# Loading expert weights in runs of 32 KB and 16 KB, with every fourth column on the other side of the product

## The reference, cut to what matters

```python
def expert_block(args):
    tok, e = args
    xb = x_pad[tok]
    gu = xb @ w_gu[e] + b_gu[e]            # w_gu[e]: 1024 x 2048 float32, 8 MB
    gate, up = gu[:, :D_FF], gu[:, D_FF:]
    gate = jnp.minimum(gate, SWIGLU_LIMIT)
    up = jnp.clip(up, -SWIGLU_LIMIT, SWIGLU_LIMIT)
    h = (up + 1.0) * gate * jax.nn.sigmoid(SWIGLU_ALPHA * gate)
    return h @ w_down[e] + b_down[e]       # w_down[e]: 1024 x 1024 float32, 4 MB
```

## Time and profile before

| | us |
|---|---|
| median of 3 runs (1173.86 to 1175.33) | 1174.92 |
| the profiled execution, its own time | 1173.83 |
| its span in the trace | 1171.8 |
| PE busy | 1109.4 |
| DVE busy | 298.5 |
| ACT busy | 151.8 |
| POOL busy | 96.4 |

### The profile page before, as it was taken

How to read it: one execution, slowest core, us unless ns; L and a number is a source line. 1 busy time by engine, 2 the same in 40 slices (tenths; PEclk the granted TensorE clock), 3 DMA queues, 4 the chain that set the end, 5 groups by cost and what they waited for, 6 DMA issues and landing times.

```text
span 1171.8 us, 13786 instructions
## 1 busy us (share of the span) xinstructions
PE 1109.4 (95%) x5376; PEld 521.9 (45%) x5376; DVE 298.5 (25%) x529; ACT 151.8 (13%) x245; POOL 96.4 (8%) x53
## 2 busy tenths in 40 slices
PE   8989999899999999999999898989899999999996
PEld 5879955535343434343434242424242424243432
DVE  3771664421212121121202020211112121212113
ACT  3242101011101011111010111111101010110101
POOL 3684420000000000000000000000000000000002
PEclk9989999899999999999999999999999999999998
DMA  9953375797999999999999999999999999999994
GB/s 355 328 187 109 118 290 197 273 422 309 419 418 415 420 415 422 413 422 413 422 413 422 413 421 414 421 414 422 413 423 413 421 414 421 415 420 415 419 417 187
DMA packets 94504, 436.10 MB, mean 372 GB/s; under 512 B 8784, under 2 KB 18768, under 8 KB 61488
## 3 DMA queue, kind: packets, MB, share of 16 engines
q1 hardware_dynamic: 87952, 428.68, 90.9%
q10 hardware_dynamic: 6528, 7.09, 1.7%
HBM read 431.78 MB, written 3.97 MB: 372 GB/s over the span
## 4 chain that ended last, share of the span: by engine, by line
PE 52%; SPq 22%; DMA 16%; DVE 6%; issue 3%; ACT 1%; DVEq 0%
PE bank L779 19%; SPq L388 13%; PE bank L796 11%; DMA ring<-w_down 9%; SPq L392 8%; DMA old_rooms<-w_down 6%; PE bank L481 5%; PE bank L737 3%; PE bank L608 3%; PE bank L862 3%; DVE zu L1113 1%; PE bank L508 1%; DVE biasp L1115 1%; PE bank L766 1%; ACT oo L988 1%
## 5 line engine op out<-in xcount | busy, mean ns | idle before, releaser
L779 PE MATMUL bank<-ring,xg 128*64 128x512 f32 x1536 | 337.2, 593 | 0.0
L779 PEld LDWEIGHTS bank<-ring,xg 128*64 128x64 f32 x1536 | 107.1, 137 | 207.7 <-issue 202.5
L796 PE MATMUL bank<-ring,act_t 128*64 128x512 f32 x768 | 176.6, 597 | 16.2 <-DMA ring<-w_down 16.1
L1399 DVE TENSOR_SCALAR gate_c<-bank 128x512 f32<-128x512 f32 x32 | 22.1, 692 | 395.1 <-PE bank L779 395.1
L779 PE MATMUL bank<-old_rooms,xg 128*64 128x512 f32 x512 | 112.8, 592 | 0.0
L796 PEld LDWEIGHTS bank<-ring,act_t 128*64 128x64 f32 x768 | 50.8, 136 | 123.2 <-issue 72.9
L737 PEld LDWEIGHTS bank<-onehot,hid 128*128 128x128 f32 x720 | 81.5, 192 | 12.2 <-issue 12.2
L1291 DVE CAST sel<-sel_all 96x128 bf16 (+1 forms) x16 | 3.6, 223 | 325.0 <-PE bank L862 325.0
L1047 POOL TENSOR_TENSOR rstd<-veps,minus_half 128x1 f32<-128x1 f32 x6 | 3.3, 548 | 986.3 <-DVE veps L1223 986.3
L737 PE MATMUL bank<-onehot,hid 128*128 128x128 f32 x720 | 84.4, 277 | 0.0
L1021 POOL TENSOR_TENSOR w_parts<-ring,w_parts 128x1024 fp32r<-128x1024 f32 x26 | 75.4, 2908 | 55.5 <-ACT w_parts L893 55.5
(11 more groups left out here) (199 smaller groups left out, 734.6 us busy)
## 6 DMA issues: line engine op xcount, KB each, us to landing
ring<-w_gu SPq DMA_DIRECT2D x192, 1024.0 KB, 24.3
ring<-w_down SPq DMA_DIRECT2D x96, 1024.0 KB, 19.7
old_rooms<-w_gu SPq DMA_DIRECT2D x64, 1024.0 KB, 20.5
old_rooms<-w_down SPq DMA_DIRECT2D x29, 1024.0 KB, 24.8
ring<-w_in SPq DMA_DIRECT2D x13, 1024.0 KB, 14.5
ring<-w_out SPq DMA_DIRECT2D x4, 1024.0 KB, 6.7
st<-s_ret SPq DMA_DIRECT2D x4, 512.0 KB, 10.8
lnp<-ln ACTq DMA_DIRECT2D x4, 512.0 KB, 7.7
```

The source lines that it names most:

```text
L779: mm = pe.matmul(bank[2 * a + n][64 * hf:64 * hf + 64, :], xg[:, c, 64 * a:64 * a + 64], w[:, col:col + 512], start=False, stop=(c == KC - 1))
L796: mm = pe.matmul(bank[4][64 * hf:64 * hf + 64, :], act_t[:, a, c % 4, 64 * (c // 4):64 * (c // 4) + 64], w[:, c % 2, hf * 512:(hf + 1) * 5 ...
L1399: dve.tensor_scalar(gate_c[:, :], bank[2 * a][:, :], LIMIT, None, ALU.min).then_inc(gate_ready, 1)
```

## The change

From pair 1 on, four neighbouring 1 MB pieces of `w_gu` become one transfer of 4 MB (`GU_RUN = 4`): rows k + 4p to k + 4p + 3 go to partition p, a run of 32 KB. Two pieces of `w_down` become one transfer of 2 MB with rows k + 4p to k + 4p + 3, a run of 16 KB (`DN_RUN = 4`). The rooms stay 16 of 1 MB; a transfer takes four or two that lie side by side. SP waits until the last of the pieces that it overwrites has been used, and PE waits once for the whole transfer (`run_landed`). Pair 0 keeps its 1 MB pieces; those of `w_down` there now give each partition two neighbouring rows, a run of 8 KB. To match, `gather` and `transpose_act` take every fourth column (every second in pair 0's `transpose_act`). The number of products, of columns and of bytes stays.

```diff
+GU_RUN, DN_RUN = 4, 4
+GU_UNITS, DN_UNITS = GU_RUN, DN_RUN // 2
...
+        def rooms(n, units):
+            r = ring[:, n:n + units, :] if n < RING else old_rooms[:, n - RING:n - RING + units, :]
+            return r.rearrange("p a b -> p (a b)")
...
+        runs = [(j, GU_UNITS) for j in range(0, 2 * GU_PIECES, GU_UNITS)] \
+            + [(j, DN_UNITS) for j in range(2 * GU_PIECES, PAIR_PIECES, DN_UNITS)]
...
-                return sp.dma_start(dst.rearrange("p (k n) -> p k n", n=D), w_down[bass.ds(e, 1), k:k + 256, :]
-                                    .rearrange("e (k p) n -> p (e k) n", p=128))
+                return sp.dma_start(dst.unsqueeze(1), w_down[bass.ds(e, 1), k:k + 256, :]
+                                    .rearrange("e (p k) n -> p e (k n)", p=128))
+
+            def expert_run(j, ea, eb, dst):
+
+                if j < 2 * GU_PIECES:
+                    e, k = (ea, eb)[j // GU_PIECES], (j % GU_PIECES) * 128
+                    return sp.dma_start(dst.unsqueeze(1), w_gu[bass.ds(e, 1), k:k + 128 * GU_RUN, :]
+                                        .rearrange("e (p k) n -> p e (k n)", p=128))
+                i = j - 2 * GU_PIECES
+                e, k = (ea, eb)[i // DN_PIECES], (i % DN_PIECES) * 256
+                return sp.dma_start(dst.unsqueeze(1), w_down[bass.ds(e, 1), k:k + 128 * DN_RUN, :]
+                                    .rearrange("e (p k) n -> p e (k n)", p=128))
...
-                for j in range(PAIR_PIECES):
+                for j, units in runs:
                     g = pair_fill(j, odd)
...
-                        sp.wait_ge(piece_used, MIX_PIECES + piece_of.get(g - WIDE, g - WIDE + len(SIDE)) + 1)
+                        sp.wait_ge(piece_used, MIX_PIECES + 1 + max(piece_of.get(m - WIDE, m - WIDE + len(SIDE))
+                                                                    for m in range(g, g + units)))
                     else:
-                        sp.wait_ge(piece_used, first + (j - WIDE + 1))
-                    expert_piece(j, ea, eb, room(g % WIDE)).then_inc(slot_full[g % WIDE], 16)
+                        sp.wait_ge(piece_used, first + (j + units - WIDE))
+                    expert_run(j, ea, eb, rooms(g % WIDE, units)).then_inc(slot_full[g % WIDE], 16)
...
-                                       hid[:, t, c * 128:(c + 1) * 128], onehot[:, t, :],
+                                       hid[:, t, :].rearrange("p (q m k) -> p q k m", m=128, k=GU_RUN)
+                                       [:, c // GU_RUN, c % GU_RUN, :], onehot[:, t, :],
...
+            def run_landed(j, units, turn, odd):
+
+                g = pair_fill(j, odd)
+                once, per_turn = run_landings(g)
+                pe.wait_ge(slot_full[g % WIDE], 16 * per_turn * turn + 16 * once)
+                return rooms(g % WIDE, units)
...
-                                      act_h[:, a, j * 128:(j + 1) * 128], ident)
+                                      act_h[:, a, :].rearrange("p (q m k) -> p q k m", m=128, k=run)
+                                      [:, j // run, j % run, :], ident)
...
-                        w = landed(2 * GU_PIECES + DN_PIECES * a + c // 2, turn, odd)\
-                            .rearrange("p (k n) -> p k n", n=D)
+                        j = 2 * GU_PIECES + DN_PIECES * a + c // 2
+                        w = landed(j) if turn is None else run_landed(j, DN_UNITS, turn, odd)
+                        w = w.rearrange("p (k n) -> p k n", n=D)
```

More of the change, by code:

```diff
@@ L300, in pair_fill, with run_landings @@
             return FIRST_FILLS + (0 if odd else PAIR_PIECES) + j
+        runs = [(j, GU_UNITS) for j in range(0, 2 * GU_PIECES, GU_UNITS)] \
+            + [(j, DN_UNITS) for j in range(2 * GU_PIECES, PAIR_PIECES, DN_UNITS)]
+        run_rooms = [pair_fill(j, odd) for odd in (True, False) for j, _ in runs]
+        def run_landings(g):
+            n = g % WIDE
+            return mixer_fills[n] + sum(m % WIDE == n for m in range(FIRST_FILLS)) \
+                + sum(m % WIDE == n and m <= g for m in run_rooms), sum(m % WIDE == n for m in run_rooms)
         def mixer_wait(eng, i):
@@ L745, in gates, with landed, transpose_act @@
                 mm.then_inc(gt_mm, 1)
[L747 to L759, removed]
-                return room(g % WIDE)
-            def transpose_act(a, p):
+            def landed(j):
+                g = first_fill(j)
+                if g is None:
+                    pe.wait_ge(side_full[j], 16)
+                    return side[j]
+                pe.wait_ge(slot_full[g % WIDE], 16 * (mixer_fills[g % WIDE] + g // WIDE + 1))
+                return room(g % WIDE)
+            def run_landed(j, units, turn, odd):
[3 more added lines that the diff above has]
+                return rooms(g % WIDE, units)
+            def transpose_act(a, p, run):
                 pe.wait_ge(act_ready, 2 * p + a + 1)
@@ L774, in gate_up @@
                         between[c]()
-                    w = landed(GU_PIECES * a + c, turn, odd)
+                    if turn is None:
+                        w = landed(GU_PIECES * a + c)
+                    elif c % GU_RUN == 0:
+                        w_run = run_landed(GU_PIECES * a + c, GU_UNITS, turn, odd).rearrange("p (k n) -> p k n", n=2 * FF)
+                    if turn is not None:
+                        w = w_run[:, c % GU_RUN, :]
                     for n in range(2):
@@ L791, in down @@
                         between[c]()
-                    if c % 2 == 0:
-                        w = landed(2 * GU_PIECES + DN_PIECES * a + c // 2, turn, odd)\
-                            .rearrange("p (k n) -> p k n", n=D)
+                    run = 2 if turn is None else DN_RUN
+                    if c % run == 0:
+                        j = 2 * GU_PIECES + DN_PIECES * a + c // 2
+                        w = landed(j) if turn is None else run_landed(j, DN_UNITS, turn, odd)
+                        w = w.rearrange("p (k n) -> p k n", n=D)
                     for hf in range(2):
@@ L797, in down @@
                                        act_t[:, a, c % 4, 64 * (c // 4):64 * (c // 4) + 64],
-                                       w[:, c % 2, hf * 512:(hf + 1) * 512], start=False, stop=(c == KC - 1))
+                                       w[:, c % run, hf * 512:(hf + 1) * 512], start=False, stop=(c == KC - 1))
                     if c % 2 == 1:
@@ L827, in pair @@
                 gate_up_bias(1)
-                gate_up(1, turn, odd, {4: lambda: transpose_act(0, p)} | ({2: count_before, 6: by_expert} if first else {}))
+                gate_up(1, turn, odd, {4: lambda: transpose_act(0, p, 2 if first else DN_RUN)} | ({2: count_before, 6: by_expert} if first else {}))
                 pe.wait_ge(act_t_ready, 2 * p + 1)
@@ L833, in pair @@
                     sums_so_far(2, 3)
-                down(0, turn, odd, {4: lambda: transpose_act(1, p)})
+                down(0, turn, odd, {4: lambda: transpose_act(1, p, 2 if first else DN_RUN)})
                 if last:
```

## The result

The changed kernel takes 1234.24 us (median of 4 runs, 1232.92 to 1235.02) against 1174.39 for the kernel before, measured beside it: ratio 1.051, 95% interval 1.049 to 1.053. It is 60 us slower, where 19 us faster was forecast, and it lies outside the range. The numbers are close to those of the first rival.

A forecast was written before the change was run, and what follows sets the result against it. The prediction took DMA transfers to bound the kernel from about 286 us on. Restart 286.9 + 4.8 + 780.4 gave the last landing at 1072.1, pair 14 19 us earlier: 1174.92 − 19 = 1156 us, range 1146 to 1188.

The forecast's parts named there:

- first rival: Strided weight loads in gather and transposes are slow: up to 5.7 us a pair, 1230 us in all; chance 0.17.
- The bound: Second half, from about 286 us: DMA transfers set the pace; faster transfers can give at most 30.6 us.
- Packets: Weight transfers: each packet costs 9 ns, so fewer, longer ones take a pair from 60.24 to 58.5 us.
- The straight line: Packet cost at 4 KB and 8 KB runs, drawn on to 16 KB and 32 KB: 58.5 us a pair.
- the rival of cut packets: Weight transfers: packets above 8 KB are cut, or cost goes by bytes; 59.7 us a pair, 1171 us; chance 0.12.
- Coarser start and end: Restart waits for two used pieces, 1.7 us later; pair end waits for a longer transfer, 1.9 us later, once.
- The two tight places: First w_gu and first w_down run of pair 2: DMA stays fed, some 3 us to spare at each.
- the rival of starved transfers: DMA runs dry as rooms come free four at a time: 1158 to 1161 us; with slower transfers, chance 0.08.
- I take none: Weight loads of gather and transpose_act on PE: reading every fourth float32 was counted as no cost.
- one step more: PE weight loads: a column starting a new memory line costs transposes 0.5 us a pair, gather nothing.
- The rival: The first rival: strided weight loads on PE are slow, 5.7 us a pair, 1230 us; chance 0.17.
- twice the time of a column: Upper end for strided weight loads: 0.110 us more per gather load, 0.057 per transpose load, 5.7 us a pair.

The follow-up runs named there:

- experiment 1: Changed kernel with its long transfers, but gather and the activation transposes take neighbouring columns again (wrong columns, same work); 1152.95 us, ratio 0.984.
- experiment 2: Kernel before with its 1 MB pieces, but gather and all activation transposes take every fourth column (wrong columns, same work); 1234.12 us, ratio 1.052.
- experiment 4: Changed kernel, but the first layer norm writes hid in run order so gather reads neighbouring columns; transposes keep every fourth; 1155.94 us, ratio 0.986.
- experiment 3: Changed kernel with runs of two rows: w_gu runs of 16 KB, w_down runs of 8 KB, every second column; 1158.07 us, ratio 0.988.
- experiment 7: As experiment 4, but DVE's norm walks the permutation with its inner loop along 128 neighbouring elements of hid, inputs at steps of four; 1155.41 us, ratio 0.985.

## Why the prediction was wrong, point by point

**The bound.** Right. The transfers set the pace of the second half: faster ones alone gave 20.1 us (experiment 1), and the 30.6 us that PE left were not exceeded.

**Packets.** Right in mechanism and size. The straight line from 4 KB and 8 KB to 16 KB and 32 KB gave 58.5 us a pair and 58.45 was measured; with runs of two it was 59.1 and 59.03. The packet counts above show that runs over 8 KB are not cut, and the rival of cut packets falls.

**Coarser start and end.** The start is right: in experiment 1 SP issues the first `w_down` run at 286.09, 3.48 us after pair 1 begins, where it was 1.76 us in the kernel before. Pair 14 ends at 1073.3 for 1075.9 forecast; of the 2.6 us, 0.8 is that pair 1 begins at 282.61 in place of 283.43, and 1.1 the 0.08 us a pair over 13.33 pairs. The two tight places held: the DMA share of experiment 1 is 1.05 from 300 to 310 us and 0.99 from 340 to 350, and the rival of starved transfers falls.

**PE: "I take none".** This is the step that failed. The prediction argued that transposes take their columns in half the time of `gather` (0.45 for 0.86 ns), so that `gather` had room for a step more per column. That `gather` had two steps a column was worked out from these rates, and no row showed that a new line could use the second one. Both rates were those of neighbouring columns, four to a line. They say how fast columns of a line come, and nothing of how fast lines do. With each column alone in its line both kinds slow down, `gather` by 137 ns a load (71%), transposes by 69 ns (49%). For the load of a transpose the "one step more" was about right (0.54 ns a column for the 0.45 of a step), though it came to 0.18 us a pair and not 0.5; for `gather`, where it was to be nothing, it was 1.07 ns a column. The change trades 1.8 us a pair on the DMA side for 11.40 − 5.55 = 5.85 us a pair of `gather` and 2 × 0.09 us of transposes on PE, and PE had 3.6 us to spare in late pairs and none in early ones. So PE, not the transfers, set the pace of every pair.

The sum by experiment 1: 15 × 5.85 + 30 × 0.09 = 90.5 us more on PE, less the 9.3 us that PE waited there for `w_gu`, is 81.2. Experiments 2 and 1, run beside each other, differ by 1234.12 − 1152.95 = 81.2 us. That the two agree to 0.1 us is partly chance, since the runs of one kernel spread over 2 to 3 us: the profiled executions of the changed kernel and of experiment 1 differ by 1235.02 − 1152.01 = 83.0. The 1.8 us more arise before pair 1, which starts 290.79 − 282.61 = 8.2 us later where 6.0 were due: the last 32 products of pair 0 take 8.76 us for 7.06, at the lower clock told under experiment 4.

**The rival.** Its price was near: 5.7 us a pair for 6.0 measured, 1230 for 1234. The upper bound, "twice the time of a column" (0.110 us a load), was too low: loads of `gather` that follow each other went from 81.5 / 720 = 113 to 169.1 / 720 = 235 ns. What was wrong with it was its chance. With no row that showed a stepped load, and `gather` without a pause in which to hide one, 0.17 was too little, and what the Trainium skill ("SBUF — State Buffer", the section on the DMA port swizzle) says of 16-byte lines spoke for it: each crossing to a new line pays. The same note lets a step of four float32 values pass as free; here that step costs 329 ns for 192, and the measurement decides. Of two reads in a line being enough the runs agree for `gather` (196 ns at a step of two) and not for transposes (208 for 140).

## What to carry to other kernels

When a layout change makes transfers better, look for who pays for the new order: here a weight load for float32 products that reads one float per 16-byte line costs 1.0 ns a column more, and it stood on the engine that had 3.6 us a pair to spare for a change that needed 6. Take the order where the data is written once (experiment 4, 1155.9 us) or shorten the runs until two columns share a line (experiment 3, 1158.1 us), before giving up the long transfers; both beat the kernel before (1173.1 us), by 1.4% and 1.2%. And a rate read from neighbouring elements is no bound for stepped ones: where a trace has no such row, measure one instruction before the whole change.

## What the runs showed of the hardware that was not expected

- Weight loads of 128 float32 columns for a float32 product take 192, 196, 261, 329 and 335 ns at steps of 1, 2, 3, 4 and 8 columns; those of transposes 140, 208, 201 and 209 ns at steps of 1, 2, 3 and 4.
- The transposes' loads grew by 69 ns each, but a group of four transposes only from 0.66 to 0.75 us, so most of it lay under the products. From the changed kernel, PE in order of time:

```profile
311.76 0.75 PE L798 MATMUL bank<-cst,act_h 128*128 128x128 f32 x4
```

- DVE's instruction on 128 x 512 float32 with a PSUM input goes from 746 to 1091 ns when it writes with steps of 128 floats, and to 1124 when it reads with steps of four.
- PE's granted clock can fall while PE works without a pause: in the changed kernel and experiments 2, 4 and 7 the last 32 products of pair 0 take 8.76 us in place of 7.06. From 264 to 274 us the granted clock is 0.83 of the upper level, 2.4 GHz, in the changed kernel and in experiment 4, and 1.00 in experiment 1. The lower level is 1.2 GHz; 1.7 us lost is an estimate of 3.4 us spent there. Just before, PE had run ten small products of 24 columns and then the bias, and the same in experiment 1, where the clock did not fall.
